# A 25th weight buffer over the expert choice's scratch in a two-layer hybrid decoder kernel

## What is computed

```python
for l in range(DEPTH):                          # DEPTH = 2
    x = mixer_block(x, positions, ...)          # RMSNorm, projections, 3 branches, gates, w_out
    x = hier_moe_block(x, ...)

def hier_moe_block(x, norm_g, w_rg, b_rg, w_re, b_re, w1, w3, w2):
    xn = rms_norm(x, norm_g).reshape(n_tok, d)
    ...   # top 1 of 4 groups, then top 2 of the 8 experts in it -> combine (n_tok, 32)
    hid = jax.nn.silu(jnp.einsum("nd,edf->nef", xn, w1)) * jnp.einsum("nd,edf->nef", xn, w3)
    hid = hid * combine[:, :, None]
    return x + jnp.einsum("nef,efd->nd", hid, w2)
```

## Time and profile before

| | us |
|---|---|
| median of 3 runs | 991.89 (991.26 to 992.02) |
| the profiled execution, its own time | 992.2 |
| its span from first to last instruction | 990.1 |
| TensorE busy, share of the span | 946.0, 96% |
| VectorE, ScalarE, GpSimd busy | 483.8, 419.2, 27.1 |

### The profile page before, as it was taken

One profiled execution on the slowest core, in us unless ns is written; L12 is line 12 of the kernel. 1 busy time (PEld: TensorE's weight loads), 2 busy tenths in 40 slices (PEclk: granted clock), 3 DMA queues, 4 the chain that ended last, 5 costly groups with the idle time before them and its releaser, 6 DMA issues.

```text
span 990.1 us, 19050 instructions
## 1 busy us (share of the span) xinstructions
PE 946.0 (96%) x8004; PEld 758.8 (77%) x8004; DVE 483.8 (49%) x894; ACT 419.2 (42%) x645; POOL 27.1 (3%) x43
## 2 busy tenths in 40 slices
PE   8999999999999999977999999999999999998886
PEld 8898899999876566544698988999998756564544
DVE  7466875477833222222273669655687422232111
ACT  7465654656542221111275565564754421211111
POOL 1011000000000000000100110000000000000000
PEclk9999999999999999989999999999999999999989
DMA  8734545557799999999975264536769999999995
GB/s 288 272 126 170 177 171 170 192 193 298 290 391 402 422 421 420 419 420 421 382 242 198 87 218 157 185 128 213 274 237 365 381 389 421 420 420 420 420 421 212
DMA packets 86310, 293.36 MB, mean 296 GB/s; under 512 B 17040, under 2 KB 17104, under 8 KB 61904
## 3 DMA queue, kind: packets, MB, share of 16 engines
q1 hardware_dynamic: 86224, 292.12, 76.8%
HBM read 291.05 MB, written 1.05 MB: 295 GB/s over the span
## 4 chain that ended last, share of the span: by engine, by line
PE 75%; DMA 14%; DVE 4%; ACT 3%; SPq 1%; issue 1%; ACTq 0%; DVEq 0%
PE ps_a L854 10%; PE ps_a L856 10%; PE ps_a L855 10%; PE ps_b L1186 9%; DMA units_over_xnT<-in_w_dram 6%; PE ps_a L838 5%; PE ps_a L840 5%; PE ps_a L839 5%; PE ps_b L1207 4%; PE ps_b L1134 3%; DMA unit_from_layer_begin<-in_w_dram 3%; DMA weight_ring<-in_w_dram 3%; DMA units_over_splits<-in_w_dram 3%; PE ps_b L1299 2%; PE ps_a L1258 2%; SPq L605 1%
## 5 line engine op out<-in xcount | busy, mean ns | idle before, releaser
L1614 DVE TENSOR_TENSOR w_low<-weight_ring,w_high 128x1024 fp32r<-128x1024 f32 x167 | 201.3, 1230 | 91.9 <-ACT w_high L1330 91.4
L1330 ACT ACTIVATE w_high<-weight_ring 128x1024 fp32r<-128x1024 f32 x166 | 173.6, 1057 | 156.4 <-PE ps_a L856 107.2
L854 PE MATMUL ps_a<-xnT_high,w_high 128*128 128x256 f32 x704 | 200.8, 285 | 0.1
L856 PE MATMUL ps_a<-xnT_high,w_low 128*128 128x256 f32 x704 | 199.0, 283 | 0.0
L855 PE MATMUL ps_a<-xnT_low,w_high 128*128 128x256 f32 x704 | 198.1, 281 | 0.0
L854 PEld LDWEIGHTS ps_a<-xnT_high,w_high 128*128 128x128 f32 x704 | 132.8, 189 | 2.4 <-issue 2.4
L855 PEld LDWEIGHTS ps_a<-xnT_low,w_high 128*128 128x128 f32 x704 | 133.1, 189 | 0.5 <-issue 0.5
L856 PEld LDWEIGHTS ps_a<-xnT_high,w_low 128*128 128x128 f32 x704 | 131.9, 187 | 0.0
L1540 ACT ACTIVATE h<-ps_b 128x256 f32<-128x256 f32 x64 | 24.5, 383 | 142.9 <-PE ps_b L1186 142.9
L1993 DVE TENSOR_TENSOR y_lo<-ps_b,y_hi 128x512 fp32r<-128x512 f32 x30 | 20.8, 692 | 105.8 <-ACT y_hi L1571 105.8
L1299 PEld LDWEIGHTS ps_b<-fold_two_matrices,h 128*128 128x128 f32 x256 | 35.0, 196 | 40.3 <-issue 36.1
(11 more groups left out here) (372 smaller groups left out, 1758.7 us busy)
## 6 DMA issues: line engine op xcount, KB each, us to landing
weight_ring<-in_w_in_dram SPq DMA_DIRECT2D x62, 1024.0 KB, 5.2
units_over_splits<-in_w_dram SPq DMA_DIRECT2D x48, 1024.0 KB, 23.1
units_over_attention<-in_w_dram SPq DMA_DIRECT2D x40, 1024.0 KB, 21.9
weight_ring<-in_w_dram SPq DMA_DIRECT2D x24, 1024.0 KB, 20.8
units_over_xnT<-in_w_dram SPq DMA_DIRECT2D x20, 1024.0 KB, 22.4
units_over_merged<-in_w_dram SPq DMA_DIRECT2D x16, 1024.0 KB, 24.3
weight_ring<-in_w_branch_dram SPq DMA_DIRECT2D x12, 1024.0 KB, 5.4
unit_from_layer_begin<-in_w_dram SPq DMA_DIRECT2D x10, 1024.0 KB, 18.4
```

The costliest lines, as they stand in the source:

```text
L854: mm(dst, wh, xh, start=row == 0 and s % 2 == 0, stop=False, skip_group_check=True)
L856: last = mm(dst, wl, xh, start=False, stop=row == rows - 1, skip_group_check=True)
L1330: A(mix_buf(whi, i), mix_raw(i), ACT.Copy).then_inc(hi_ready, 1)
L1614: v.tensor_tensor(mix_buf(wlo, i), mix_raw(i), mix_buf(whi, i).bitcast(F32), ALU.subtract).then_inc(lo_ready, 1)
```

## The change

A 25th place, `unit_over_choice`, is laid over the choice's scratch. The scratch has 4,192 bytes a partition left of the mixer region `one` behind four units, and a unit needs 8,192; so behind that region now lie, in this order, the tensors that a unit of layer one may overwrite: `tri`, `neg_mask`, `trineg_r`, `negones_r`, the router weights and bias, the convolution weights and `index_i`. Unit 24 becomes the fourth `ONCE_UNITS` entry. SyncE loads it behind unit 23, when the first `select_weighted` is written, and before it reads the rounds. GpSimd makes the four constants again in layer two, with eight instructions and a wait for the tenth `w_low`; TensorE and VectorE wait for them (`begun` at 11) ahead of their first use.

What the experts need during their work and what lay in that scratch moves too: `silu_h1`, `h3_weighted`, `hid0` and `h` go to where `selectT0` was, `hid1` behind y. `selectT0` moves over the once-used place of unit 5. So it may be written only after unit 5 was used: its copy goes from pair 0 to pair 1 (`first_selT_out`), and there `outputs(0)` now comes ahead of the `gather` instead of behind it.

```diff
-ONCE_UNITS = (4, 5, 23)
+ONCE_UNITS = (4, 5, 23, 24)
+CONSTANTS_AGAIN = 11
...
+    once_choice = Region(nc, one_b.at, whole.at).sb("unit_over_choice", [P, UNIT])
...
-    t.once = [once_y[:, :], once_XT1[:, :], once_x[:, :]]
+    t.once = [once_y[:, :], once_XT1[:, :], once_x[:, :], once_choice[:, :]]
...
         if p == 0:
             steps.extend((("first", 0), ("first", 1)))
-            steps.append(("first_selT", 0))
             selecting.extend((1, piece, 0) for piece in range(3))
+        elif p == 1:
+            steps.append(("first_selT_out", 0))
+            outputs(p - 1)
+            gather()
...
                 load_unit(sp, ONCE_UNITS[2])
+                sp.wait_ge(selw_ready, 1)
+                load_unit(sp, ONCE_UNITS[3])
...
+    def constants_again(pool):
+
+        def below(buf, row, fill):
+            nc.gpsimd.affine_select(out=buf[:, :], in_=buf[:, :], compare_op=ALU.is_ge, fill=fill, base=0,
+                                    pattern=[[row, P]], channel_multiplier=-row).then_inc(begun, 1)
+
+        nc.gpsimd.memset(t.tri[:, :], -1.0).then_inc(begun, 1)
+        nc.gpsimd.memset(t.neg_mask[:, :], 0.0).then_inc(begun, 1)
+        pool.wait_ge(begun, 5)
+        nc.gpsimd.tensor_copy(t.negones_r[:, :], t.tri[:, :]).then_inc(begun, 1)
+        below(t.neg_mask, -1, NEG)
...
+        if l:
+            pool.wait_ge(lo_ready, 10)
+            constants_again(pool)
...
             if p:
                 pe.wait_ge(ylo_done, p)
             else:
-                pe.wait_ge(first_taken, 2)
+                pe.wait_ge(first_taken, 1)
...
-                elif what == "first_selT":
+                elif what == "first_selT_out":
                     act.wait_ge(first_given, 2)
+                    act.wait_ge(unit_used, used[ONCE_UNITS[1]])
```

More of the change, by code:

```diff
@@ L153, in tensors @@
     t.x = sb("x_res", [P, NT, D])
-    t.ident, t.tri = (sb(n, [P, P]) for n in ("ident", "tri"))
-    t.neg_mask, t.ones = (sb(n, [P, P]) for n in ("neg_mask", "ones"))
-    t.trineg_r, t.negones_r = (sb(n, [P, P], F32R) for n in ("trineg_r", "negones_r"))
+    t.ident, t.ones = (sb(n, [P, P]) for n in ("ident", "ones"))
     t.eps, t.junk = sb("eps", [P, 1]), sb("junk", [P, 1])
-    t.fold, t.index, t.index_i = sb("fold", [P, SLOTS]), sb("index", [P, NE]), sb("index_i", [P, NE], I32)
+    t.fold, t.index = sb("fold", [P, SLOTS]), sb("index", [P, NE])
     t.fold_two = sb("fold_two_matrices", [P, 2 * SLOTS])
@@ L167, in tensors @@
     t.msum = sb("sum_sq_both", [P, NT])
-    t.wr, t.br = sb("w_router", [P, NK, NR]), sb("b_router", [P, NR])
     t.tri_bf, t.ones_bf = sb("tri_strict_bf", [P, P], BF16), sb("ones_bf", [P, P], BF16)
@@ L190, in tensors @@
     t.tri_strict = one.again().sb("tri_strict", [P, P])
+    sb = whole.sb
+    t.tri, t.neg_mask = (sb(n, [P, P]) for n in ("tri", "neg_mask"))
+    t.trineg_r, t.negones_r = (sb(n, [P, P], F32R) for n in ("trineg_r", "negones_r"))
+    t.wr, t.br = sb("w_router", [P, NK, NR]), sb("b_router", [P, NR])
+    t.convw, t.convr = sb("conv_w", [P, 4 * 2 * NC]), sb("conv_rows", [4 * 2 * NC, P])
+    t.index_i = sb("index_i", [P, NE], I32)
     one_b = one.again()
@@ L193, in tensors @@
     units_one = sb("units_over_attention", [P, 4, UNIT])
-    t.act1, t.u = sb("silu_h1", [P, 2, SLOTS]), sb("h3_weighted", [P, 2, SLOTS])
+    once_choice = Region(nc, one_b.at, whole.at).sb("unit_over_choice", [P, UNIT])
     t.lg = sb("logits", [P, NT, NR])
@@ L199, in tensors @@
     t.oh1, t.oh2 = (sb(n, [P, NT, NE]) for n in ("first_pick", "second_pick"))
-    after_choice = one_b.again()
     t.tops, t.top_at = sb("top_logits", [P, NT, NG, EPG]), sb("top_places", [P, NT, NG, EPG], U32)
@@ L203, in tensors @@
     t.most = sb("most_tokens", [P, 2])
-    t.hid = [after_choice.sb(f"hid{i}", [P, 2, 2, SLOTS]) for i in range(2)]
-    t.h = after_choice.sb("h", [P, FE])
     two = whole.part(73728)
@@ L223, in tensors @@
     once_XT1 = r.again().sb("unit_over_XT1_selectT", [P, UNIT])
-    XT1, selT1 = r.sb("XT1", [P, NK, BATCH * SLOTS]), r.sb("selectT1", [P, HALF, SEQ], F32R)
-    r.part(4 * UNIT - 4 * NK * BATCH * SLOTS - 4 * HALF * SEQ)
+    XT1 = r.sb("XT1", [P, NK, BATCH * SLOTS])
+    t.selT = [r.sb(f"selectT{i}", [P, HALF, SEQ], F32R) for i in range(2)]
     t.wif, t.ifT = r.again().sb("w_if", [P, NK, SLOTS]), Region(nc, r.at + 1024, two.end).sb("if_by_feature", [P, SEQ])
@@ L258, in tensors @@
     t.softplus_hi, _, t.softplus_lo = (r.sb(n, [P, 4, 384], F32R) for n in ("softplus_high", "softplus_r", "softplus_low"))
-    t.convw, t.convr = sb("conv_w", [P, 4 * 2 * NC]), sb("conv_rows", [4 * 2 * NC, P])
     sb = spare.sb
@@ L277, in tensors @@
     t.x_squares = r.again().sb("x_squares", [P, CHUNK])
-    t.selT = [sb("selectT0", [P, HALF, SEQ], F32R), selT1]
+    t.act1, t.u = sb("silu_h1", [P, 2, SLOTS]), sb("h3_weighted", [P, 2, SLOTS])
+    t.hid = [b("hid" + i, [P, 2, 2, SLOTS]) for b, i in ((sb, "0"), (y_at.sb, "1"))]
+    t.h = sb("h", [P, FE])
     t.ps_a = ctx.enter_context(nc.psum_tensor("ps_a", [P, 4, 512], F32))
@@ L768, in run_sync @@
             sp.wait_ge(stored, 64)
+    def constants_again(pool):
[7 more added lines that the diff above has]
+        below(t.neg_mask, -1, NEG)
+        pool.wait_ge(begun, 7)
+        below(t.tri, -1, 0.0)
+        pool.wait_ge(begun, 8)
+        nc.gpsimd.tensor_copy(t.trineg_r[:, :], t.tri[:, :]).then_inc(begun, 1)
+        pool.wait_ge(begun, 9)
+        nc.gpsimd.memset(t.tri[:, :], 1.0).then_inc(begun, 1)
+        pool.wait_ge(begun, 10)
+        below(t.tri, 1, 0.0)
     def run_gpsimd(pool):
@@ L804, in run_gpsimd @@
             pool.wait_ge(unit_in[PLACES - 1], 16)
-            pool.wait_ge(unit_in[place_of(ONCE_UNITS[2])], 16)
+            pool.wait_ge(unit_in[place_of(ONCE_UNITS[3])], 16)
             for run in t.mixer_sems.runs():
@@ L906, in sb_cumsum @@
             pe.wait_ge(sb_split, 2 * (g + 1))
+            if l and not g:
+                pe.wait_ge(begun, CONSTANTS_AGAIN)
             for hh in range(4):
@@ L1690, in masked @@
         def masked(row0, row1):
+            if l:
+                dve.wait_ge(begun, CONSTANTS_AGAIN)
             nm = bc(t.neg_mask[:, :], 1, 4)
```

## The result

The changed kernel takes 983.25 us (981.93 to 985.84), the kernel before 991.95 us on the same chip, six runs each: ratio 0.9904 [0.9886, 0.9922]. By that ratio it is 9.5 us faster; the two medians alone differ by 8.7. The forecast was 2.0 us and its range ended at 988.2, so the prediction was wrong, in size and not in sign. The profiled execution took 983.43 us, its span is 981.7 (before 990.1).

What follows compares the result with a forecast made beforehand. The prediction took weight loads by DMA to bound each layer's experts, with gains only where the queue runs dry. It summed 0.4 + 1.6 = 2.0 us off, giving 989.9 us, range 988.2 to 992.4 (likeliest case 988.6 to 991.0).

Steps and rivals of the forecast that it cites:

- What bounds the kernel: Experts of each layer: they end when the last byte has come, so one more place gains only where the queue runs dry.
- The load of unit 24: Start of each layer's experts: issued 0.4 us earlier, worth 0.2 us a layer, 0.4 us in all.
- The depth behind it: Experts, after unit 24: each later unit is issued one place earlier, filling the second dry stretches, 1.60 us.
- the second stretches: Low DMA rate at 314 to 318 us (layer one) and 803 to 808 (layer two), losing 0.40 and 1.20 us.
- SyncE's reading of the rounds: Now after unit 24's issue: if it takes 1 us, unit 25 goes out a little later, at a cost of 0.
- The constants: Layer two, GpSimd: eight instructions, 2.3 us, at most 13, with some 18 us of slack, cost 0.
- The copy of selectT: Pair 1, ScalarE: 0.60 us between the third `h` and `y_hi`, hidden, costing nothing at the end.
- the last sentence before the sum: Memory layout: router weights, convolution weights and expert scratch only change address, 0, with no row for an address that matters.
- The signs that the prediction had named for being right: Earlier loads of units 24 and 28, second stretches at 415 GB/s or more, GpSimd done before 526, layer two's experts 1 us shorter.
- The slowest engine is never dry: Rival, dry stretches: only faster DMA engines waited, so the gain is at most 0.4 us; 991.7 us, chance 0.27.
- The slowest engine gains more than the mean: Rival, dry stretches: the slowest DMA engine lost more than the mean, gain 4.2 us; 987.7 us, chance 0.14.
- One engine falls behind once more: Rival, experts: one more late landing in each layer and none of the gain, 994.9 us; chance 0.09.

Runs made afterwards that it cites:

- e3: The changed kernel without the 25th place and its load, all else kept: 983.88 us, ratio 0.9906 to the kernel before.
- e2: The changed kernel, unchanged, run again as a control: 983.23 us, ratio 0.9903 to the kernel before.
- e4: The kernel before with only the new order in pair 1 (copy of selectT, outputs of pair 0, then gather): 990.75 us, ratio 0.9979.
- e13: The changed kernel with the gather ahead of the outputs of pair 0 again, 25th place kept: 983.47 us, ratio 0.9918 to the kernel before.
- e5: The kernel before with 32 unused bytes ahead of the upper part of SBUF: 989.49 us, ratio 0.9963.
- e7: The changed kernel with 32 unused bytes ahead of the upper part of SBUF: 986.62 us, ratio 0.9945 to the kernel before.
- e1: The kernel before, unchanged, run again as a control: 993.28 us, ratio 0.9997.
- e8: The changed kernel with the lower part of SBUF also started at a multiple of 256 bytes: 980.92 us, ratio 0.9885 to the kernel before.
- e10: The changed kernel with all unit places at multiples of 256 bytes and the split weights 64 bytes later: 971.67 us, ratio 0.9791 to the kernel before.

## Why the prediction was wrong

*What bounds the kernel* was read rightly: each layer's experts end with the last byte. But "it can gain only where the queue runs dry" left out two things: how fast a full queue moves, and how long the mixers take in which TensorE is never idle.

*The load of unit 24.* The lead of 0.4 us came as forecast (5.62 and 5.61 us after unit 23's issue, before 6.07 and 6.06). Whether it is worth the 0.4 us in all can't be told: e3 against e2 doesn't resolve it.

*The depth behind it.* The forecast took 1.60 us for the second stretches. They closed, and e4 measured 2.1 us [0.8, 3.4] for the order alone: 1.60 lies in that interval. The share was not known: "this helps the same second stretch" is what e3, e4 and e13 show, each part alone is enough.

*SyncE's reading of the rounds* lies in the 1.34 us between the issues of units 24 and 25 (301.31 to 302.65), and 1.66 us in layer two; before, units 24 and 25 went out 0.38 us apart. That is near the 1 us that was set at 0.

*The constants* were right to the tenth. GpSimd's timeline, first and last of the eight, then its next own work:

```profile
511.60 0.21 POOL L783 MEMSET tri<- 128x128 f32 x1 [15.39 <-DVE w_low L1647]
...
513.60 0.29 POOL L780 TENSOR_SCALAR_AFFINE_SELECT tri<-tri 128x128 f32<-128x128 f32 x1
...
541.99 3.21 POOL L825 TENSOR_SCALAR_AFFINE_SELECT attn_b<-attn_b 128x512 f32<-128x512 f32 x2 [28.10 <-DVE attn_b L1670]
```

They take 2.3 us and end 28.1 before it. The copy of selectT takes 0.59 us between an `h` and a `y_hi`, as forecast, for nothing:

```profile
308.37 0.38 ACT L1572 ACTIVATE h<-ps_b 128x256 f32<-128x256 f32 x1 [1.75 <-PE ps_b L1218]
308.64 0.59 ACT L1580 ACTIVATE selectT<-ps_b 128x512 fp32r<-128x512 f32 x1
310.08 0.60 ACT L1604 ACTIVATE y_hi<-ps_b 128x512 fp32r<-128x512 f32 x1 [0.84 <-PE ps_b L1239]
```

*The step that failed* is the last sentence before the sum: the tensors "only change address: 0, with no row for an address that matters". No run shows a cost of the tensors named there; but taking them out of the front of memory moved the lower part by 3,520 bytes down and the upper by 608 up. That changed the distance of the mixer's operands from 96 to 128 and set the upper part at a multiple of 256. The first gave 0.56 us in 80, or 1.6 to 2.0 us in each mixer, 3.5 in all (e5, which does this alone, 3.7 us [1.8, 5.6]). The second gave 0.022 us for each of some 72 units in a layer, 3.2 us in all (taking it away, e7 against e2, cost 3.4 by the medians and 4.2 by the ratios, although the mixers were 0.9 us shorter in e7's profile). With 2.1 us for the stretch that is 8.8 of the 9.6 us of e2. This is a sum of parts from different runs; that they add up in one program is argued.

The end of the kernel, from the last landing on, was 1.4 us shorter in the first pair of profiles and 0.7 between e1 and e2. It doesn't follow the program: it took 9.5 to 11.0 us over all sixteen, and 10.5 in e3 against 9.6 in e2.

The signs that the prediction had named for being right came, apart from the absolute times of the load over the choice, which went out earlier still. They all look at the queue, and none at TensorE's pace or at the rate of a full queue.

*The rivals* all had the wrong cause. "The slowest engine is never dry" falls with e4, which gained from the stretch. "The slowest engine gains more than the mean" rested on 23.2 us between the landings of units 23 and 31 in layer two. The control e1 has 21.7 there with its stretch dry, and e13 has 23.1 with its stretch full, since two units landed 4.1 and 4.0 us after the one before them. So an excess of that size comes without a dry queue, too. "One engine falls behind once more" named something real, late landings, that is alike in all programs: among the landings 40 to 94 those over 2.7 us exceed 2.46 us by 1.0 to 2.8 us together in a layer, in every kernel, and by some 1.6 in most. The true rival, that a layout moves the rates by which every term was priced, was not on the list: a term set at 0 for want of a row should have widened the range upward and downward.

## What to carry to other kernels

When a change moves tensors, work out the start address of everything that a DMA writes or TensorE reads, before and after, and compare over 256 bytes; a padding of 32 to 192 bytes is a one-line experiment and can outweigh the change itself. Place large DMA destinations at multiples of 256 bytes, and where TensorE is the bound, try the distance between its two operands, too, since no rule here gives the best one. And before a change is credited, undo its named part alone: here it was worth nothing that could be measured.

## What was not expected of the hardware

- Matmuls of fp32r from two SBUF operands ran at a pace that went by the operands' distance: 79.79 us at distance 0 and 77.46 at 192 (e8, e10) for the same instructions, 2.9%. Two executions of one program differed by 0.01 us (the kernel before, 79.81 and 79.80) and by 0.11 us (the changed one, 79.35 and 79.24), two programs of one layout at 192 by 0.41. The granted clock was 1.00 in 150 to 230 us of every run. It doesn't look like interference of other engines: the mean distance of the 256-column matmuls' starts in the table's stretch with VectorE and ScalarE both idle was 119.7 ns in e1 and 118.8 in e2 (46 starts each), with one of them busy 119.9 and 118.8. That it is a conflict between loading weights and streaming is argued, not shown. The Trainium skill rules such a conflict out (*TensorE: Matmul & The Clock Gate*, section on what each phase of a matmul is for: the next tile's weight load takes no SBUF read bandwidth from the running matmul). The measured dependence on the two operands' distance stands against that for these shapes and this type, or has another cause that no run here shows.
- With the roles exchanged (split weights loaded, x moving), distance 0 was the fastest of those that were tried: a mean of 394 ns (high by high) and 389 (high by low) in e8 against 401 and 396 in e1. No single distance is best for both forms.
- The pace of the experts' matmuls was untouched: 86.8 us in e1 and in e2 between the same two starts, near 316 and 403 in e1.
